# Two runs of small records at a time, then two gate eighths, in the solve's levels

## What the kernel computes

```python
def step(S, inp):
    r_t, w_t, k_t, v_t, a_t, b_t = inp
    Sa = jnp.einsum("bhvk,bhk->bhv", S, a_t)
    S = S * w_t[:, :, None, :] + Sa[..., None] * b_t[:, :, None, :] + v_t[..., None] * k_t[:, :, None, :]
    y = jnp.einsum("bhvk,bhk->bhv", S, r_t)
    return S, y
...
gate_a, gate_b = jnp.split(jax.nn.sigmoid(h @ w_gate[i] + b_gate[i]), 2, axis=-1)
merged = gate_a * (y_a @ w_branch_a[i]) + gate_b * (y_b @ w_branch_b[i])
```

## Time and profile before

| | us |
|---|---|
| median of 3 runs | 955.06 (954.5 to 955.4) |
| the profiled execution, its own time | 956.54 |
| its span in the profile | 954.70 |

### The profile page before, as it was taken

The page is one execution under the profiler, slowest core; times in us unless marked ns, Lnnn a source line. Parts: engine busy times, 40 slices in busy tenths (PEclk is TensorE's granted clock), DMA queues, the critical chain, the costliest instruction groups (busy, mean ns, idle before and its releaser), DMA issues.

```text
span 954.7 us, 15908 instructions
## 1 busy us (share of the span) xinstructions
PE 933.7 (98%) x6783; PEld 769.9 (81%) x6783; DVE 409.4 (43%) x645; ACT 428.6 (45%) x683; POOL 384.9 (40%) x180
## 2 busy tenths in 40 slices
PE   6999999999999999999999999999999999999996
PEld 5887888897778778788788888888888888888885
DVE  4223798308565548559244434434344300100435
ACT  6355553235554644623445344443444411412647
POOL 2453444442223526246423444444444444445350
PEclk9999999999999999999999999999999999999998
DMA  7432433332121000226412333333333332323132
GB/s 250 129 92 64 110 88 90 88 90 67 45 59 33 27 25 25 68 71 216 134 44 67 89 106 93 92 107 89 103 96 90 110 110 99 100 89 119 63 105 89
DMA packets 115163, 86.59 MB, mean 91 GB/s; under 512 B 2852, under 2 KB 100022, under 8 KB 115094
## 3 DMA queue, kind: packets, MB, share of 16 engines
q1 hardware_dynamic: 114904, 85.50, 30.3%
q10 hardware_dynamic: 190, 0.08, 0.0%
HBM read 83.47 MB, written 2.10 MB: 90 GB/s over the span
## 4 chain that ended last, share of the span: by engine, by line
PE 95%; ACT 2%; DVE 1%; POOL 1%; DMA 1%; issue 0%; SPq 0%; DVEq 0%
PE bank L544 19%; PE bank L545 18%; PE bank L546 18%; PE bank L606 9%; PE bank L607 9%; PE bank L608 9%; PE bank L863 2%; PE bank L734 1%; PE bank L771 1%; PE bank L819 1%; PE bank L748 1%; POOL w_lo L524 1%; DMA xs<-in_x_dram 1%; PE bank L860 1%; PE bank L904 0%; PE bank L830 0%
## 5 line engine op out<-in xcount | busy, mean ns | idle before, releaser
L524 POOL TENSOR_TENSOR w_lo<-raw,w_hi 128x1024 fp32r<-128x1024 f32 x137 | 330.5, 2412 | 490.4 <-ACT w_hi L1144 490.3
L1144 ACT ACTIVATE w_hi<-raw 128x1024 fp32r<-128x1024 f32 x137 | 145.4, 1061 | 339.6 <-issue 201.2
L544 PE MATMUL bank<-hT_hi,w_hi 128*128 128x512 f32 (+1 forms) x720 | 282.1, 392 | 1.2 <-POOL w_lo L524 1.0
L546 PE MATMUL bank<-hT_hi,w_lo 128*128 128x512 f32 (+1 forms) x720 | 277.0, 385 | 0.0
L545 PE MATMUL bank<-hT_lo,w_hi 128*128 128x512 f32 (+1 forms) x720 | 277.0, 385 | 0.0
L544 PEld LDWEIGHTS bank<-hT_hi,w_hi 128*128 128x128 f32 x720 | 135.2, 188 | 29.3 <-issue 1.7
L546 PEld LDWEIGHTS bank<-hT_hi,w_lo 128*128 128x128 f32 x720 | 135.3, 188 | 27.1
L545 PEld LDWEIGHTS bank<-hT_lo,w_hi 128*128 128x128 f32 x720 | 135.4, 188 | 25.1
L2052 DVE SCALAR_TENSOR_TENSOR cbuf<-bank,params,cbuf 128x511 f32<-128x511 f32 x48 | 36.0, 750 | 132.9 <-ACT cbuf L1542 132.9
L606 PE MATMUL bank<-w_hi,g_hi 128*128 128x512 f32 x184 | 71.7, 390 | 0.0
L608 PE MATMUL bank<-w_hi,g_lo 128*128 128x512 f32 x184 | 71.6, 389 | 0.0
(11 more groups left out here) (318 smaller groups left out, 1350.4 us busy)
## 6 DMA issues: line engine op xcount, KB each, us to landing
raw<-in_w_up_dram SPq DMA_DIRECT2D x48, 512.0 KB, 3.8
raw<-in_w_in_dram SPq DMA_DIRECT2D x33, 512.0 KB, 4.0
raw<-in_w_down_dram SPq DMA_DIRECT2D x24, 512.0 KB, 3.8
raw<-in_w_gate_dram SPq DMA_DIRECT2D x16, 512.0 KB, 4.0
raw<-in_w_out_dram SPq DMA_DIRECT2D x8, 512.0 KB, 4.1
raw<-in_w_ple_gate_dram SPq DMA_DIRECT2D x8, 512.0 KB, 4.2
xs<-in_x_dram SPq DMA_DIRECT2D x4, 512.0 KB, 5.3
raw<-in_w_branch_a_dram SPq DMA_DIRECT2D x4, 512.0 KB, 3.4
```

What stands on the lines that cost most here:

```text
L524: nc.gpsimd.tensor_tensor(low(n)[:, :], raw[:, n % RAW_SLOTS, :], high(n)[:, :].bitcast(F32), ALU.subtract).then_inc(*step("pool", ("lo", n)))
L544: nc.tensor.matmul(o, wh, ah, start=first, stop=False)
L546: return nc.tensor.matmul(o, wl, ah, start=False, stop=last)
L1144: nc.scalar.activation(high(u)[:, :], raw[:, u % RAW_SLOTS, :], ACT.Copy) \
```

## The change

Within each half round the two runs now stand one behind the other, and the two eighths follow them together. No product is added or taken away, and the other engines' code is the same.

```diff
             for lv in range(1, 5):
                 level_both(0, lv, 2, lv - 1)
-                gate_parts(1)
                 level_both(1, lv, 3, lv - 1)
-                gate_parts(1)
+                gate_parts(2)
                 if lv < 4:
                     (with_r_and_a, tokens_of_keys, with_r_and_a)[lv - 1]((0, 0, 2)[lv - 1])
                 level_both(2, lv, 0, lv)
-                gate_parts(1)
                 level_both(3, lv, 1, lv)
-                gate_parts(1)
+                gate_parts(2)
                 if lv < 3:
                     (with_r_and_a, tokens_of_values)[lv - 1]((1, 0)[lv - 1])
```

## The result

| | us |
|---|---|
| before, median of 22 runs | 954.79 (953.18 to 955.8) |
| after, median of 22 runs | 956.07 (954.26 to 957.74) |
| ratio, 95% interval | 1.0012 (1.0007 to 1.0018) |
| profiled execution of after | 955.63, span 953.8 |

The change makes the kernel 1.3 us slower; the interval leaves out 1, so this is small but not noise. The two profiled spans (954.7 and 953.8) say the opposite, and this is the first thing to read rightly: the profile of before began late. TensorE's first product of the solve starts 2.0 us later in it (295.65 against 293.63), long before any changed instruction. So the stretch of the solve is compared, from its first product to its last: 47.88 us before, 48.57 after. One profile each gives only 0.7 us; with the second profile of each kernel (further down: 46.98 and 48.97) the means are 47.4 and 48.8, which is the 1.3 us.

A forecast was written before the change was run, and what follows sets the result against it. TensorE's issued work was taken to bound the kernel. Joints saving 2.6 us and pauses adding 1.5 gave -1.1 us, so 954.0 from the median of before, stated as 953.9; range 952.3 to 955.8.

The forecast's parts named there:

- What bounds the kernel: Whole kernel: the sum of what TensorE issues sets the end; savings reach it unless a later wait takes them.
- Terms 1 and 2: Each half round: paired eighths save 0.23 us, adjoining runs 0.09; together 0.32, or 2.6 us over eight.
- the narrow place: Second half round of level 2: TensorE may wait for ScalarE's `Wp` copies; 0 to 0.3 us once, taken as 0.
- Term 3: Second run of each half round: its copies are done in time, so no wait is added; taken as 0.
- Rival B: Half rounds following a copy of products: ScalarE's lateness replaces the eighths, losing 1.2 us; 955.1, no change; chance 0.13.
- Term 4: Instruction packets in the loop: 1.0 us more at the first pause, 0.5 more at the eight behind; 1.5 us added.
- Rival C: Pairs of runs: packets bind and the stock runs out in each; 960.5, or 956.5 with half of it; chance 0.06.
- rival A: Packet crossings in the loop: refills stay hidden or today's pauses are chance; full 2.6 us gained, 952.5; chance 0.19.

The follow-up runs named there:

- with 192: The changed kernel with 192 do-nothing instructions (waits already met) added ahead of the solve, the first ahead of TensorE's first transposes; 973.24 us.
- the diluted kernels: Kernels before and after, each run cut to 5 of 8 column blocks with a 256-column product in its middle; 955.51 us (order of before), 952.65 (changed order).

## Why the prediction was wrong

**What bounds the kernel** was right: the sum of what TensorE does, no later wait took it back, and the difference made in the solve stood at the end (1.3 us between the mean solves, 1.3 us in the times). I had passed over one wait as large as the two of rows 2, for VectorE at L656 ahead of the solve; it is 1.1 us before and 1.2 after, so it changes nothing.

**Terms 1 and 2, the joints,** had the right sum: 0.32 us for each half round was measured (3.58 for 3.90), and 2.6 us in all: without their pauses and the narrow place the two solves last 47.88 - 1.36 = 46.5 and 48.57 - 4.57 - 0.08 = 43.9 us. The split was luck in part: the eighths save 1.78 - 1.59 = 0.19 us where I had 0.23, and the runs 2.12 - 1.99 = 0.13 where I had 0.09 and a bound of 0.11.

**Term 3, the waits,** was right: the narrow place in level 2 costs 0.08 us (0.73 for 0.65), and nothing else in the levels waits. Rival B is out for this kernel.

**Term 4, the instructions,** is the step that failed, in its second part. At the first packet, which I walked through, the pause was to grow by 1.0 us. It was 0.95 and 1.33, against 0.70 and 0.24 before, so by the means it grew by 0.7. For the eight behind it I took 200 instructions in hand, a chance of one in five for each to lie badly, and 0.65 us for each that does: 1.0 us in all, 0.5 more than before. Measured are 3.6 us of pauses behind the first, in both profiles, against 0.7 and 0.25: four of the eight packets pay, 0.55 to 1.04 us each. So both the share and the size were too small.

Two things were wrong in it. First, I had measured only from a packet's start on the queue to its code (2.3 to 2.9 us) and treated the start as given. But in the profiles of both kernels each next packet of the loop starts 0.3 to 3.1 us after the code of the last one has begun to run, so a pause delays the next packet too. What counts is the whole time from code to code. Where it is 3.9 to 4.0 us, as in level 4, two runs and two eighths (268 instructions in 3.58 us, so 256 in 3.4) can't go at their own pace, wherever the packet begins in them; with products of 0.65 or 1.09 us between the pairs, as in levels 2 and 3, they mostly can. It isn't 3.9 us everywhere: it was 3.4 ahead of 5825, and with 192 level 4 got through with 0.38 us and paid behind it. Second, 1.57 us of eighths were to cover what falls outside a pair; but at 5825 the stock ran out one product into the eighths, and they covered nothing.

With the measured terms the sum is right: 2.6 saved, pauses from 0.9 to 4.7 (means of two profiles each), so 3.8 lost where I had 1.5, 1.2 slower; 1.3 was timed. Rival C had the mechanism, the point from which it decides (0.32 us of added pause for each half round; it was 0.48), and a price near the time (956.5 if half of it comes; 956.07 was timed), but a chance of only 0.06. For rival A I had leaned on the Trainium skill, "Runtime: NRT & Kernel Launch", section "Instruction fetch mechanics": that a crossing is mostly hidden. It holds in these runs for the diluted kernels, and in the profile of after for the stretch of 512-column products from 601.0 to 657.7 us, where a packet lasts 28.3 us and TensorE has no idle moment; it does not for runs of small float32 products. That the range was too narrow has the same root: its upper end, 955.8, left out nearly all of C.

Why it took 5.37 us from 4289 to 4545, in both profiles, is open. What the traces do tell is that the packet itself was not slow (2.3 us from its start to its code); it started late, 3.1 and 3.0 us behind the code at 4289, at records 4362 and 4359. In both profiles of before it starts at 4362 and 4360 as well, 2.3 us behind, so the place in the program has a part in it. Open too is why the runs of the changed kernel scatter more than those of before (954.26 to 957.74 against 953.18 to 955.8). A fallen clock would do it, but no profile of it shows one, and the granted clocks of its 22 runs (0.996 to 0.999) don't order them: 0.996 stands beside 956.06 and beside 957.74, and 957.13 has 0.999.

## What to carry to other kernels

Count instructions as a resource of their own: where TensorE issues many small products, divide 256 by their pace and compare it with the time from one packet's code to the next, here 3.4 to 4.0 us where TensorE had to wait for it, and once 5.4. A change between small and large products costs some 0.16 us here (0.32 for the two that went in each half round), but the slow products that stand between fast runs also give the next packet time to come; here gathering them cost 3.8 us of pauses and saved 2.6. And compare a stretch, not the span, when two profiles begin differently: the span here had the wrong sign.

## What the runs showed of the hardware

- TensorE's instructions come in packets of 256 on one queue. In stretches of small products 3.4 to 4.0 us passed from the start of one packet's code to that of the next, once 5.4. In the four profiles of the two kernels the next packet started 0.3 to 3.1 us after the last one's code had begun to run, and its own code ran 2.2 us after its start at the earliest. The pauses stand at one remainder of the record count, in every profile that has any.
- A wait that is already met isn't free for TensorE. 64 instructions of two such waits each stand 0.11 us apart (from 4.9 to 11.7 us). Part of that hides behind the first inputs: 64 of them delayed the solve by 4.0 us, 192 by 17.7.
- After idle stretches of 1.62 and 1.36 us inside the loop the granted clock fell from 1.00 to 0.50; after one of 1.37 us it didn't, nor after those of up to 1.04 us in the two profiles of the changed kernel.
